# A hybrid decoder trunk on one core: x sigmoid(x) from Exp, add, reciprocal and multiply, or from Tanh and one operation

## What is computed

```python
h = rms_norm(x, norm_g)
p = jnp.einsum('btd,dp->btp', h, w_in)
...
ya = gla_mixer(aq, ak, av, alr, ...) * jax.nn.silu(az)
yb = swa_mixer(bq, bk, bv, ...) * jax.nn.silu(bz)
yc = diff_mixer(cq, ck, cv, ...) * jax.nn.silu(cz)
yd = gdn_mixer(dqkv, dbeta, da, ...) * jax.nn.silu(dz)
return x + jnp.einsum('btm,md->btd', jnp.concatenate([ya, yb, yc, yd], -1), w_out)
```

## Time and profile before

| what | before |
|---|---|
| median of three runs | 2127.36 us |
| the profiled execution's own time | 2127.9 us |
| its span (first to last instruction) | 2126.1 us |
| mean granted TensorE clock | 0.989 of full speed |
| PE busy | 2038.3 us (96%) |
| POOL busy | 1396.3 us (66%) |
| DVE busy | 1026.4 us (48%) |
| ACT busy | 537.6 us (25%) |
| chain that ended last | PE 72%, DVE 20%, ACT 5%, rest 3% |
| largest line of that chain | PE L421, 55% of the span |

### The profile page before, as it was taken

How to read it: one execution, slowest core, us unless ns; L and a number is a source line. 1 busy time by engine, 2 the same in 40 slices (tenths; PEclk the granted TensorE clock), 3 DMA queues, 4 the chain that set the end, 5 groups by cost and what they waited for, 6 DMA issues and landing times.

```text
span 2126.1 us, 25561 instructions
## 1 busy us (share of the span) xinstructions
PE 2038.3 (96%) x10300; PEld 1660.6 (78%) x10300; DVE 1026.4 (48%) x1407; ACT 537.6 (25%) x1014; POOL 1396.3 (66%) x1164
## 2 busy tenths in 40 slices
PE   7998999999999989999999999999999999999999
PEld 6877878878888878767888778778778787776777
DVE  1699453453222455565427984435432225545563
ACT  4010221222222443332320112221222225423220
POOL 6797654555777756557787975545557777555676
PEclk9999999999999999999999999999999999999999
DMA  5232211211222211422442322111122222132223
GB/s 216 74 96 80 70 60 50 60 60 60 80 81 88 80 60 63 146 69 80 129 132 72 99 79 63 57 60 59 51 62 87 80 80 84 55 127 81 74 85 119
DMA packets 50709, 175.92 MB, mean 83 GB/s; under 512 B 5566, under 2 KB 6304, under 8 KB 49568
## 3 DMA queue, kind: packets, MB, share of 16 engines
q1 hardware_dynamic: 44288, 155.75, 23.3%
q10 hardware_dynamic: 6304, 18.55, 2.3%
HBM read 165.89 MB, written 8.39 MB: 82 GB/s over the span
## 4 chain that ended last, share of the span: by engine, by line
PE 72%; DVE 20%; ACT 5%; issue 2%; DMA 1%; SPq 0%; ACTq 0%
PE acc L421 55%; DVE slots L1256 3%; DVE slots L1199 3%; DVE general L1263 3%; PE mix L488 2%; PE mix L499 1%; PE mix L682 1%; PE mix L660 1%; PE mix L528 1%; PE mix L491 1%; DVE slots L1252 1%; ACT slots L849 1%; DVE general L1319 1%; DVE slots L1429 1%; PE mix L774 1%
## 5 line engine op out<-in xcount | busy, mean ns | idle before, releaser
L376 POOL TENSOR_TENSOR w_hi<-w_raw,zeros 128x512 fp32r<-128x512 f32 x576 | 626.2, 1087 | 671.5 <-PE acc L421 648.2
L421 PE MATMUL acc<-w_hi,actT_hi 128*128 128x512 f32 x1920 | 789.0, 411 | 14.0 <-DVE slots L1232 12.1
L380 POOL TENSOR_TENSOR w_lo<-w_raw,w_hi 128x512 fp32r<-128x512 f32 x576 | 767.6, 1333 | 45.1
L421 PE MATMUL acc<-w_hi,actT_lo 128*128 128x512 f32 x1920 | 755.3, 393 | 0.0
L421 PE MATMUL acc<-w_lo,actT_hi 128*128 128x512 f32 x1920 | 753.5, 392 | 0.0
L421 PEld LDWEIGHTS acc<-w_hi,actT_hi 128*128 128x128 f32 x1920 | 364.9, 190 | 106.6 <-issue 38.7
L421 PEld LDWEIGHTS acc<-w_hi,actT_lo 128*128 128x128 f32 x1920 | 363.2, 189 | 80.3
L421 PEld LDWEIGHTS acc<-w_lo,actT_hi 128*128 128x128 f32 x1920 | 365.3, 190 | 65.5
L421 PE MATMUL acc<-actT_hi,w_hi 128*128 128x512 f32 x384 | 153.2, 399 | 2.9 <-DVE slots L1232 2.9
L421 PE MATMUL acc<-actT_hi,w_lo 128*128 128x512 f32 x384 | 150.4, 392 | 0.0
L421 PE MATMUL acc<-actT_lo,w_hi 128*128 128x512 f32 x384 | 150.4, 392 | 0.0
(11 more groups left out here) (250 smaller groups left out, 2095.5 us busy)
## 6 DMA issues: line engine op xcount, KB each, us to landing
w_raw<-in_wstream SPq DMA_DIRECT2D x288, 512.0 KB, 3.5
out_x<-slots ACTq DMA_DIRECT2D x7, 1024.0 KB, 4.4
slots<-in_x SPq DMA_DIRECT2D x4, 1024.0 KB, 14.5
slots<-in_x ACTq DMA_DIRECT2D x1, 4096.0 KB, 14.2
slots<-out_x ACTq DMA_DIRECT2D x1, 4096.0 KB, 15.0
out_x<-slots ACTq DMA_DIRECT2D x4, 256.0 KB, 2.3
cf_sb<-in_cf ACTq DMA_DIRECT2D x1, 964.0 KB, 11.4
slots<-in_masks ACTq DMA_DIRECT2D x1, 384.0 KB, 12.2
```

The source lines that it names most:

```text
L376: pool.tensor_tensor(w_hi[:, r], w_raw[:, s, k], zeros[:, :].broadcast_to([P, GW]), ALU.add) \
L380: pool.tensor_tensor(w_lo[:, r], w_raw[:, s, k], w_hi[:, r].bitcast(F32), ALU.subtract).then_inc(w_ready, 1)
L421: last = nc.tensor.matmul(acc[b][:, :], lhsT, rhs, start=(k == 0 and i == 0), stop=(k == kts - 1 and i == 2))
```

## The change

Both silus get the form (x/2)(1 + tanh(x/2)). ACT's Exp with scale -1 becomes Tanh with scale 1. DVE's add, reciprocal and multiply become one scalar_tensor_tensor, (tanh + 1) times x/2. The halves come from elsewhere: the convolution's taps are halved once at the start, so that its result is already x/2, and the four gate chunks are scaled by `xr_half` instead of `xr` when ACT empties them; `xr_half` is one small DVE operation per layer, put right after the wait for `xr` and before the four `rd` steps. The steps g1, g2, one and rec go from the lists; `half` comes in.

```diff
@@ take_out (ACT)
-                    nc.scalar.activation(slot(SLOT[c])[:, b], acc[b][:, :], ACT.Copy, scale=xr[:, l, b:b + 1]) \
+                    r = (xr_half if c in GATES else xr)[:, l, b:b + 1]
+                    nc.scalar.activation(slot(SLOT[c])[:, b], acc[b][:, :], ACT.Copy, scale=r) \
                         .then_inc(acc_free, 1)
@@ conv_gate (ACT)
-                        nc.scalar.activation(general[:, b % 2], slot(CONV[c])[:, b], ACT.Exp, scale=-1.0) \
+                        nc.scalar.activation(general[:, b % 2], slot(CONV[c])[:, b], ACT.Tanh) \
@@ the gate of a GDN tile (ACT); GLA, SWA and DIF alike
-                    nc.scalar.activation(U["GATE"], gz, ACT.Exp, scale=-1.0).then_inc(*s("gate"))
+                    nc.scalar.activation(U["GATE"], gz, ACT.Tanh).then_inc(*s("gate"))
@@ lambdas (DVE, once)
-                dve.wait_ge(lam_steps, 2 * DEPTH + 5)
+                taps = pcol_all[:, :, PC["conv"]:]
+                dve.tensor_scalar(taps, taps, 0.5, None, ALU.mult).then_inc(lam_steps, 1)
+                dve.wait_ge(lam_steps, 2 * DEPTH + 6)
@@ gate (DVE)
-                dve.tensor_scalar(tmp, tmp, 1.0, None, ALU.add).then_inc(St.sem, St.one(f"{t}.g1"))
-                dve.wait_ge(St.sem, St.at(l, f"{t}.g1"))
-                dve.reciprocal(tmp, tmp).then_inc(St.sem, St.one(f"{t}.g2"))
-                dve.wait_ge(St.sem, St.at(l, f"{t}.g2"))
-                dve.tensor_tensor(Zs, Zs, tmp, ALU.mult).then_inc(St.sem, St.one(f"{t}.g3"))
+                dve.scalar_tensor_tensor(Zs, tmp, 1.0, Zs, ALU.add, ALU.mult).then_inc(St.sem, St.one(f"{t}.g3"))
@@ the start of a layer (DVE)
                 dve.wait_ge(X_ACT.sem, X_ACT.at(l, "r"))
+                dve.tensor_scalar(xr_half[:, l], xr[:, l], 0.5, None, ALU.mult).then_inc(*si("half"))
@@ conv (DVE)
-                        dve.tensor_scalar(general[:, b % 2], general[:, b % 2], 1.0, None, ALU.add) \
-                            .then_inc(*ci("one"))
-                        cw("one")
-                        dve.reciprocal(general[:, b % 2], general[:, b % 2]).then_inc(*ci("rec"))
-                        cw("rec")
-                        dve.tensor_tensor(dst, dst, general[:, b % 2], ALU.mult).then_inc(*ci("mul"))
+                        dve.scalar_tensor_tensor(dst, general[:, b % 2], 1.0, dst, ALU.add, ALU.mult) \
+                            .then_inc(*ci("mul"))
```

More of the change, by code:

```diff
@@ L33 @@
 CHUNKS = ["dq", "dk", "dv", "dz", "bz", "az", "aq", "av", "bq", "bkv", "cq", "ck", "cv", "cz"]
+GATES = ("dz", "az", "bz", "cz")
 OUT_GROUPS = [3, 0, 1, 2]
@@ L95 @@
 GDN_DVE = ("ag red qn kn qd kb ke ei es0 es1 es2 es3 mt qk xi x1 xt2 x2 xt3 x3 xt4 x4 xt5 x5 xt6 xt7 "
-           "g1 g2 g3 ub v00 v01 v02 v03 s00 s01 s02 s03 v10 v11 v12 v13 s10 s11 s12 s13 redo y0 y1 y2 y3").split()
+           "g3 ub v00 v01 v02 v03 s00 s01 s02 s03 v10 v11 v12 v13 s10 s11 s12 s13 redo y0 y1 y2 y3").split()
 GLA_PE = "u cum dec tr a us o".split()
 GLA_ACT = "abs e l eb enb er dect qkT gate sqo0 sqo1 lno ro".split()
-GLA_DVE = "g qd ki ke at0 at1 s00 s01 s10 s11 g1 g2 g3 redo y0 y1 y2 y3".split()
+GLA_DVE = "g qd ki ke at0 at1 s00 s01 s10 s11 g3 redo y0 y1 y2 y3".split()
 SWA_PE = "tr s0 s1 pt0 pt1 pv".split()
 SWA_ACT = "gate qT kT p0 p1 p2 p3 es PT0".split()
-SWA_DVE = "b0 b1 b2 b3 mx mxs nm es g1 g2 g3 den rd PT1 y0 y1 y2 y3".split()
+SWA_DVE = "b0 b1 b2 b3 mx mxs nm es g3 den rd PT1 y0 y1 y2 y3".split()
 PREP_PE = "q k".split()
@@ L110 @@
 DIF_DVE = [x for h in H for x in (f"b{h}0", f"b{h}1", f"m{h}0", f"m{h}1", f"r{h}", f"c{h}", f"w{h}")] + \
-    "g1 g2 g3 os redo y0 y1 y2 y3".split()
+    "g3 os redo y0 y1 y2 y3".split()
 def hybrid_trunk(nc, x, wstream, wsmall, pcol, prow, wlr, cf, masks, out):
@@ L150, in hybrid_trunk @@
         xr = sb("xr", [P, DEPTH, TILES])
+        xr_half = sb("xr_half", [P, DEPTH, TILES])
         def slot(n):
@@ L274, in hybrid_trunk @@
                       [f"yhi{k}" for k in range(KT)])
-        S_DVE = Steps(sem("setup_dve"), ["ss"] + [f"rd{t}" for t in T] + ["smT", "b1", "beta", "nbeta", "av", "sp",
+        S_DVE = Steps(sem("setup_dve"), ["ss", "half"] + [f"rd{t}" for t in T] + ["smT", "b1", "beta", "nbeta", "av", "sp",
                                                                     "glog", "gA", "zero_gdn"] +
@@ L278, in hybrid_trunk @@
         CONV_DVE = Steps(sem("conv_dve"), [f"{c}{b}{s}" for c in ("dq", "dk", "dv") for b in range(4)
-                                           for s in ("t3", "t2", "t1", "t0", "one", "rec", "mul")])
+                                           for s in ("t3", "t2", "t1", "t0", "mul")])
         CONV_ACT = Steps(sem("conv_act"), [f"{c}{b}" for c in ("dq", "dk", "dv") for b in range(4)])
@@ L1008, in _ @@
                     gz = slot(SLOT["az"])[:, t].rearrange("p (h c) -> p h c", h=HEADS)
-                    nc.scalar.activation(V["GATE"], gz, ACT.Exp, scale=-1.0).then_inc(*s("gate"))
+                    nc.scalar.activation(V["GATE"], gz, ACT.Tanh).then_inc(*s("gate"))
                     w(A_PE, "o")
@@ L1056, in _ @@
                     nc.scalar.activation(W["GATE"], slot(SLOT["bz"])[:, t].rearrange("p (h c) -> p h c", h=HEADS),
-                                         ACT.Exp, scale=-1.0).then_inc(*s("gate"))
+                                         ACT.Tanh).then_inc(*s("gate"))
                     w(B_PE, "tr")
```

## The result

The changed kernel takes 2078.89 us (median of four runs, 2078.69 to 2083.87), the kernel before beside it 2126.53 (2125.17 to 2127.44): a ratio of 0.9782 with a 95% interval of [0.9765 to 0.9799], 47.6 us less. Forecast were 2087.0 in a range of 2073 to 2103.

A forecast was written before the change was run, and what follows sets the result against it. PE, busy 96% of the span, was taken as the bound, so time is won only where it idles or runs slowly. 29.5 us of idle plus 13.1 of clock less 2 for POOL, 40.6, gave 2087 from 2127.4; range 2073 to 2103.

The forecast's parts named there:

- SWA: PE's six waits at L660: ACT's table loads are nearly as late as the reciprocal, so 4.8 of 20.0 us go.
- The price of the new operation: DVE's single operation per gate or convolution block: 1.35 us, ends 0.7 and 1.8, read from neighbour L1256; 203 us less DVE.
- Convolution, 15.0 and 5.5: PE's four waits at L421 for emptied accumulators: all 15.0 us go, and 5.5 us of low clock behind them.
- GDN, 6.6: PE's eight waits at L528 behind the gate: all 6.6 us go.
- L451 stays: PE's six waits at L451 hang on the last normalisation, with no late gate behind it: their 10.9 us stay.
- DIF, 3.1: The adds behind the gate end earlier and the chain moves by 1.55 us, 3.1 in both layers; 3.6 idle stays at L682.
- The clock: Low clock behind PE's idles: 13.1 us come back, 5.5 in the convolution, 2.5 and 5.1 in SWA.
- rival A: The clock comes back everywhere, behind DIF's idle too: 50.9 us less 0 to 2, 2077; chance 0.20.
- POOL, 2: POOL's weight splitting falls behind PE in the convolution projections: 1 us lost a layer, 2 in all, ends 0 and 10.
- Rival D: Slower: POOL, slowed by shared SBUF access, bounds the dk, dv and dz projections; 2147 at 3.5 us a k-tile; chance 0.02.
- Rival C: Tanh brings a table load on both sides, on the chain of its gate, 2.6 us more ACT; about 2110; chance 0.05.
- Rival B: SWA's wins and the clock there don't come, and POOL starves PE in the convolution: 2102; chance 0.19.

The follow-up runs named there:

- gla_old: The changed kernel with the eight GLA gates back in the old form (Exp, add, reciprocal, multiply): 2079.78 us, 0.9786 of the kernel before.
- gdn_old: The changed kernel with the eight GDN gates back in the old form (Exp, add, reciprocal, multiply): 2087.93 us, 0.982 of the kernel before.
- extra_two: The changed kernel plus one unread DVE multiply of two SBUF tensors in each of the 24 convolution blocks: 2087.91 us, 0.982 of the kernel before.
- psum: The changed kernel with ACT writing the convolution's tanh into a free PSUM bank, so DVE reads one SBUF and one PSUM tensor: 2078.75 us, 0.9778.

## Why the prediction was right, and where it was off

**The reading of what bounds it** held: the gain is PE's idle and the low clock behind it, 31.4 + 16.7 us; gla_old shows that DVE's busy time alone counts for nearly nothing. The total was 7.5 us short of the 48.1, and the terms are off by more than that: SWA 4.4, the clock 3.6 and POOL 2.0 too low, DIF 1.7 too high, and the 0.8 that L474 cost wasn't in the sum.

**The price of the new operation** was taken at 1.35 us and is 0.80 and 0.86, inside the ends of 0.7 and 1.8. It was read from a neighbour, L1256, that is 1.44 us in the trace after, so the neighbour was a poor one. DVE's busy time fell by 225.6 instead of 203 us, which changed little, as the work lies where PE doesn't wait.

**Convolution, 15.0 and 5.5**: right, both in the traces; the 0.8 at L474 comes with it and was not foreseen. **GDN, 6.6**: right in the trace, and gdn_old gives 6.6 + 2.4, the 2.4 being clock elsewhere. **L451 stays**: right, 10.9.

**SWA is the term that was mis-sized**: "of 20.0 us just 2 x 2.4 = 4.8 go". It was 9.2. That ACT's chain would take over was right. The timeline after, of the three tiles of the earlier trace rows:
```profile
734.36 0.22 ACT L1044 ACTIVATE stat<-stat 128x16 f32<-128x16 f32 x1
734.60 1.81 DVE L1427 TENSOR_TENSOR slots<-slots,stat 128x512 f32<-128x512 f32 x2 [0.49 <-ACT stat L1044]
736.90 1.13 PE L662 MATMUL mix<-slots 128*128 128x128 f32 x8 [1.08 <-DVE slots L1459]
...
759.72 2.36 DVE L1427 TENSOR_TENSOR slots<-slots,stat 128x512 f32<-128x512 f32 x2 [1.13 <-ACT stat L1044]
...
790.42 1.29 DVE L1427 TENSOR_TENSOR slots<-slots,stat 128x512 f32<-128x512 f32 x2 [1.28 <-ACT stat L1044]
```
The pair starts within 0.03 us of the end of ACT's Exp, as forecast. But it then takes 1.81, 2.36 and 1.29 us where the earlier trace rows have 3.19, 2.35 and 2.13; I had carried these over unchanged. PE's idles became 1.08, 2.88 and 1.47 instead of 2.5, 2.9 and 2.3. These multiplies read two tensors of SBUF, and in the three tiles after they take 0.68 to 1.75 us each. Beside them is POOL:
```profile
759.79 1.74 POOL L382 TENSOR_TENSOR w_lo<-w_raw,w_hi 128x512 fp32r<-128x512 f32 x1
...
791.07 1.54 POOL L378 TENSOR_TENSOR w_hi<-w_raw,zeros 128x512 fp32r<-128x512 f32 x1 [0.79 <-PE acc L423]
```
The second multiply of the second tile starts inside this `w_lo` and takes 1.75 us; in the third tile the first one meets POOL for only 0.04 us and takes 0.69, and the second is just ahead of this `w_hi`, which takes 1.54 us instead of the 1.04 that it has undisturbed. So the shorter gate moved the pair against POOL's operations, and the pair's time moved with it. That a shift alone does this was read from the traces and not tested by a run.

**DIF, 3.1**: only 1.4 appears. The adds came early as forecast, PE's idle of 0.69 went in both layers, and the chain behind was 1.6 us earlier up to `redo`. Then y0 to y3 took longer:
```profile
882.47 2.10 DVE L1523 SCALAR_TENSOR_TENSOR slots<-slots,stat 128x128 f32<-128x128 f32 x4 [2.44 <-ACT stat L1130]
885.56 1.65 PE L684 MATMUL mix<-slots 64*128 64x384 f32 x4 [4.44 <-DVE slots L1493]
```
2.10 us, where the trace of before has 1.46 for the same four: 0.64 of the 1.55 in each layer. It is the first of the four alone, 1.32 us instead of 0.67; POOL is busy beside it for 1.17 us, before for 0.52. The idle of 4.44 stayed (3.6 was forecast). The rest, about 0.2 us in each layer, isn't explained.

**The clock**: 16.7 instead of 13.1. I had taken half of the idles below 2.96 us as without a low stretch; it came out as five of six, since two idles in each layer were much shorter than forecast. Of the two idles of 2.88 one was followed by 0.50 and one was not, so what this term came out at is in part luck: other executions with the same idles have another sum (last section). DIF's stretches stayed, by which rival A is false; it ended nearer (2077) than the forecast, though by a different sum.

**POOL, 2**: the mechanism is there and the cost near nothing, 1.5 us of waits of the weight load in four places. The prediction let POOL lose 2.7 us in each projection without a pause. In the trace the lead goes from 5.7 to 3.6 in dk, back to 5.1, to 1.7 in dv, back to 3.4, and to 0.05 in dz: POOL loses 2.2 to 3.4 us while DVE is in the convolution and wins 1.6 to 1.7 back while DVE waits for PE. At 0.05 us nothing is left of the lead, and extra_two shows that one more such operation in each block costs 9.0. Rival D's mechanism is real, and the kernel stopped just short of it. **Rival C** is false by the loads; the trace has no load beside Tanh. Of what the Trainium skill ("ScalarE: Activation LUTs", Table sets) says, the trace bears out that tanh and exp share a set, and not that Ln and Exp do: each Exp after a Ln still has its load of 1283 ns. **Rival B** is false by L662, which halved.

## What to carry to other kernels

Price a shorter operation by the waits that end on it, and for each ask what is next late in the same queue: in SWA it was a reciprocal, then another engine's table loads, then the queue's own multiplies, and only moving the one copy that PE waited for ahead of it all ended the wait (10.6 us, on top of the 20.5 for the reciprocal). Look for such an order first: by the rows of the kernel before, it could have ended SWA's wait without the new form. Durations of operations that read two tensors from SBUF (here 0.68 to 1.8 us for one shape) don't carry over once the work beside them has moved. When a long operation that reads one tensor is removed, look at the lead of the engine that had been working undisturbed in its shadow, and give one operand to PSUM if the lead is gone.

## What the runs showed that was not expected

An idle of 2.88 us of PE is followed by the lower clock in layer 0, at 762.5, and the same idle at the same place of layer 1 by none. The window there, after:
```profile
1790.00:1796.00 6.00, 4.61 (x29) 4.16 (x30) 2.37 (x6) 0.49 (x1) 1.13 (x2) 1.00 0.25 89
```
In the trace of psum, with the same idles, both layers have the stretch. And the same idle of 4.44 us was followed by 3.4 us at 0.50 in one kernel and by 6.8 in another. The profiled execution of gla_old shows how far this goes. Its waits of PE behind other engines are within 0.1 us those of the changed kernel, yet all four stretches in SWA and DIF are there and are 6.8 us long:
```profile
761.70:768.50 6.80, 5.87 (x22) 5.42 (x23) 1.90 (x6) 0.00 (x0) 0.00 (x0) 0.50 0.25 77
884.60:891.40 6.80, 4.70 (x11) 2.98 (x12) 5.82 (x15) 1.30 (x4) 0.19 (x1) 0.50 0.00 0
1792.50:1799.30 6.80, 6.04 (x22) 5.56 (x23) 1.74 (x6) 0.00 (x0) 0.00 (x0) 0.50 0.25 77
1915.40:1922.20 6.80, 4.84 (x12) 3.09 (x13) 5.68 (x15) 1.31 (x4) 0.04 (x1) 0.50 0.01 2
```
PE is busy for 21.45 us in them against 9.42, which costs 6.0 us; this execution took 2084.43, the other three of the same kernel 2079.64 to 2079.90. The changed kernel has such an execution too, 2083.87 at a mean granted clock of 0.993 beside three of 2078.69 to 2079.08 at 0.997. So the low clock behind unchanged idles moves one execution by some 5 us, and a term of the clock is to be read from several.
